# mLSTM phase of a hybrid decoder step: gated output made in four column pieces between units, six dense chunks of the last head pair held back, another matmul order in a unit

## The reference, cut to what matters

```python
def mlstm_mixer(xn, w_in, b_i, b_f, head_gain, w_out, C0, n0, m0, chunk):
    proj = (xn @ w_in).astype(F32)
    q, k, v, o, ig, fg = jnp.split(proj, cuts, axis=-1)
    ...
    h, C, n, m = mlstm_chunkwise(q, k, v, log_i, log_f, C0, n0, m0, chunk)
    h = h * lax.rsqrt(jnp.mean(h * h, axis=-1, keepdims=True) + EPS) * head_gain
    out = (jax.nn.sigmoid(o) * h.reshape(B, S, H * DV)).astype(xn.dtype) @ w_out
```

## Time and profile before

| | |
|---|---|
| median of three runs | 2530.48 us |
| profiled execution, its own time | 2529.18 us |
| its span | 2527.4 us |
| PE busy | 2442.5 us (97%), 15530 matmul instructions |
| DVE busy | 1164.1 us (46%) |
| ACT busy | 651.7 us (26%) |
| POOL busy | 160.1 us (6%) |
| chain that ended last | PE 90%, DVE 5% |

### The profile page before, as it was taken

How to read it: one execution, slowest core, us unless ns; L and a number is a source line. 1 busy time by engine, 2 the same in 40 slices (tenths; PEclk the granted TensorE clock), 3 DMA queues, 4 the chain that set the end, 5 groups by cost and what they waited for, 6 DMA issues and landing times.

```text
span 2527.4 us, 36895 instructions
## 1 busy us (share of the span) xinstructions
PE 2442.5 (97%) x15530; PEld 2330.6 (92%) x15530; DVE 1164.1 (46%) x2023; ACT 651.7 (26%) x1080; POOL 160.1 (6%) x208
## 2 busy tenths in 40 slices
PE   6999999997999999999999999999999999999998
PEld 6889898887999999999999977869999999999997
DVE  5545545566434334333336665466433333333333
ACT  3232222233212112112113354253212112112113
POOL 3000000002000000000002011012000000000002
PEclk8999999998999999999999999999999999999999
DMA  3212121101111111111111311101111111111111
GB/s 104 50 36 64 47 65 37 43 22 39 42 51 42 43 51 45 41 50 51 42 49 55 96 30 49 34 18 34 43 50 51 43 43 50 43 50 43 42 51 69
DMA packets 177416, 120.55 MB, mean 48 GB/s; under 512 B 23623, under 2 KB 173044, under 8 KB 177220
## 3 DMA queue, kind: packets, MB, share of 16 engines
q1 hardware_dynamic: 177108, 118.10, 16.0%
q10 hardware_dynamic: 144, 0.02, 0.0%
HBM read 110.94 MB, written 12.33 MB: 49 GB/s over the span
## 4 chain that ended last, share of the span: by engine, by line
PE 90%; DVE 5%; ACT 1%; issue 1%; DMA 1%; POOL 1%; SPq 0%; DVEq 0%; ACTq 0%
PE acc L1592 59%; PE acc L1672 5%; PE acc L1674 4%; PE acc L1673 4%; PE acc L1869 3%; PE acc L1871 3%; PE acc L1870 3%; PE acc L1888 1%; PE acc L1911 1%; PE acc L1899 1%; PE acc L1728 1%; DVE w_lo L1032 1%; PE acc L1695 1%; DVE rstd L1050 1%; PE acc L1713 1%
## 5 line engine op out<-in xcount | busy, mean ns | idle before, releaser
L1592 PE MATMUL acc<-x_hi,w_hi 128*128 128x352 f32 x1560 | 341.0, 327 | 15.4 <-DVE x_lo L1038 6.6
L1063 DVE TENSOR_TENSOR x_res<-x_res,acc 128x1056 f32<-128x1056 f32 x128 | 160.4, 1253 | 413.6 <-PE acc L1592 413.6
L683 ACT ACTIVATE w_hi<-w_raw 128x1024 fp32r<-128x1024 f32 x180 | 189.2, 1051 | 609.4 <-PE acc L1592 527.6
L1592 PE MATMUL acc<-x_lo,w_hi 128*128 128x352 f32 x1560 | 338.0, 325 | 0.0
L1592 PE MATMUL acc<-x_hi,w_lo 128*128 128x352 f32 x1560 | 337.8, 324 | 0.0
L1592 PE MATMUL acc<-h_hi,w_hi 128*128 128x352 f32 x1536 | 332.1, 324 | 0.0
L1592 PE MATMUL acc<-h_hi,w_lo 128*128 128x352 f32 x1536 | 331.1, 323 | 0.0
L1592 PE MATMUL acc<-h_lo,w_hi 128*128 128x352 f32 x1536 | 330.6, 323 | 0.0
L1592 PEld LDWEIGHTS acc<-x_hi,w_hi 128*128 128x128 f32 x1560 | 266.9, 190 | 18.7 <-issue 13.6
L1592 PEld LDWEIGHTS acc<-x_hi,w_lo 128*128 128x128 f32 x1560 | 269.6, 189 | 0.0
L1592 PEld LDWEIGHTS acc<-x_lo,w_hi 128*128 128x128 f32 x1560 | 266.7, 189 | 0.0
(11 more groups left out here) (265 smaller groups left out, 3103.5 us busy)
## 6 DMA issues: line engine op xcount, KB each, us to landing
w_raw<-in_w_up SPq DMA_DIRECT2D x64, 512.0 KB
w_raw<-in_w_down SPq DMA_DIRECT2D x64, 512.0 KB
w_raw<-in_w_mlstm_in SPq DMA_DIRECT2D x24, 512.0 KB
x_in<-in_x_prompt SPq DMA_DIRECT2D x8, 512.0 KB, 3.9
w_raw<-in_w_mlstm_out SPq DMA_DIRECT2D x8, 512.0 KB
w_raw<-in_w_q SPq DMA_DIRECT2D x16, 256.0 KB
w_raw<-in_w_attn_out SPq DMA_DIRECT2D x16, 256.0 KB
out_y_prompt<-y_out SPq DMA_DIRECT2D x8, 512.0 KB, 2.6
```

The lines of the kernel that those rows point to most:

```text
L683: nc.scalar.activation(w_hi[:, s.parity], w_raw[:, s.parity], ACT.Copy).then_inc(hi_split, 1)
L1063: V.tensor_tensor(blocks(x_res[:, k]), blocks(x_res[:, k]), group(o), ALU.add).then_inc(out_taken, 1)
L1592: last = T.matmul(out[:, b], w[:, k, m], x[:, TN * b:TN * b + TN], start=(k == 0 and i == 0), stop=(k == k_chunks - 1 and i == 2))
```

## The change

The six last chunks of the last pair (`HELD`) leave its windows and run after its units, before its own `out` slabs. The gated output is made in four pieces of columns (0:384, 384:768, 768:1024, samples), each by `gate`, `y_high`, `y_low`; `y_hi` gets two buffers. In the last `out` slabs DVE prepares row r-1 behind the sum of row r. On PE `part1`, `part2` and the sample unit's `part3` issue the same matmuls in another order.

```diff
+HELD = 6
+PIECES = [slice(0, 3 * LC), slice(3 * LC, 6 * LC), slice(6 * LC, SEQ), slice(SEQ, TOK)]
 def window(pr, step):
-    lo, n = PERIOD[pr], PERIOD[pr + 1] - PERIOD[pr]
+    lo, n = PERIOD[pr], PERIOD[pr + 1] - PERIOD[pr] - (HELD if pr == NPAIR - 1 else 0)
...
# ACT
-                def y_high(v):
+                def y_high(i):
+                    act.wait_ge(y_done, 4 * pr + i + 1)
                     for e in range(2):
...
                     if c == NCH:
-                        if pr > 0:
-                            act.wait_ge(blk_ready, evacuated(("out", pr - 1, 1)))
-                        act.wait_ge(y_done, 2 * pr + 1)
-                        y_high(slice(0, SEQ))
+                        y_high(2)
                     dense(window(pr, 3 * c + 5))
-                act.wait_ge(y_done, 2 * pr + 2)
-                y_high(slice(SEQ, TOK))
+                    if c in (6, 7):
+                        y_high(0 if c == 6 else 1)
+                y_high(3)
...
-            dense(range(PERIOD[NPAIR], PERIOD[NPAIR] + 8))
+            dense(range(PERIOD[NPAIR] - HELD, PERIOD[NPAIR] + 8))
# DVE, in dense
                             mark(x_final)
-                            prepare(1, FFN0, row)
+                            if row > 0:
+                                prepare(1, FFN0, row - 1)
+                            if row == KD - 1:
+                                prepare(1, FFN0, row)
# DVE, in units
                         heads_out(c - 1)
-                    update(c)
                     if c == NCH:
                         dve.wait_ge(ht_taken, t0 + NCH)
-                        dve.wait_ge(sig_done, 2 * pr + 2)
-                        gate(slice(0, SEQ))
+                        gate(2)
+                    update(c)
                     dense(window(pr, 3 * c + 4))
                     normalise(c)
+                    if c in (6, 7):
+                        dve.wait_ge(ht_taken, t0 + c)
+                        dve.wait_ge(sig_done, 2 * pr + 2)
+                        gate(0 if c == 6 else 1)
+                    if c in (7, 8):
+                        y_low(0 if c == 7 else 1)
                     if c + 2 < NT:
                         exponents(c + 2)
...
                 heads_out(NCH)
                 dve.wait_ge(ht_taken, t0 + NT)
-                gate(slice(SEQ, TOK))
-                y_low(slice(0, SEQ), 2 * pr + 1)
-                y_low(slice(SEQ, TOK), 2 * pr + 2)
+                gate(3)
+                y_low(2)
+                y_low(3)
...
+            dense(range(PERIOD[NPAIR] - HELD, PERIOD[NPAIR]))
             dve.wait_ge(n_ready, 1)
# PE, in dense
-                            pe.wait_ge(yl_ready, 2 * pr + 2)
+                            pe.wait_ge(yl_ready, 4 * pr + 3)
...
+                        if kind == "out" and k == 0 and b == 2:
+                            pe.wait_ge(yl_ready, 4 * pr + 4)
# PE, part1
                     T.transpose(acc[0:n, 0, 0:P], own[:, 1, cc], ident[:])
                     for e in range(2):
-                        T.matmul(acc[0:n, 0, P + P * e:P + P * e + n], head_sel[:, e, 0:n], mx_all[:, cc], start=True, stop=True)
+                        T.transpose(acc[0:n, 2, P * e:P * e + P], own[:, 2 + e, cc], ident[:])
                     for e in range(2):
-                        x = T.transpose(acc[0:n, 2, P * e:P * e + P], own[:, 2 + e, cc], ident[:])
+                        x = T.matmul(acc[0:n, 0, P + P * e:P + P * e + n], head_sel[:, e, 0:n], mx_all[:, cc], start=True, stop=True)
# PE, part2
-                    pe.wait_ge(a_ready, t + 1)
                     pe.wait_ge(v_ready, t + (2 if c + 1 < NT else 1))
                     if c > 0:
                         pe.wait_ge(c_ready, t)
                     if t > 0:
+                        pe.wait_ge(i_ready, t)
+                    if c < NCH:
+                        for e in range(2):
+                            h = slice(DK * e, DK * e + DK)
+                            T.matmul(acc[0:n, 2 + e, 0:DV + 1], own[h, 0, cc], c_aug[pr % 2][h], start=True, stop=True)
+                    pe.wait_ge(a_ready, t + 1)
+                    if t > 0:
                         pe.wait_ge(nd_ready, t)
-                        pe.wait_ge(i_ready, t)
                     for e in range(2):
                         x = T.matmul(acc[0:P, 0, P + (DV + 1) * e:P + (DV + 1) * (e + 1)], amat[0:n, e], v_aug[0:n, c % 2, e],
                                      start=True, stop=True)
-                    if c < NCH:
...
# PE, part3 of the sample unit: (e outer, b inner) becomes (b outer, e inner)
-                        for b in range(DEC_B):
-                            T.matmul(acc[h, 2 + b // 4, DV * (b % 4):DV * (b % 4) + DV], kw_b[:, b, h], v_aug[0:n, c % 2, e, 0:DV],
-                                     start=True, stop=True)
-                        x = T.matmul(acc[h, 1, 0:DEC_B], k_w[0:n, c % 2, h], s_rows[:], start=True, stop=True)
+                    else:
+                        for b in range(DEC_B):
+                            for e, h in enumerate(halves):
+                                T.matmul(acc[h, 2 + b // 4, DV * (b % 4):DV * (b % 4) + DV], kw_b[:, b, h],
+                                         v_aug[0:n, c % 2, e, 0:DV], start=True, stop=True)
+                        for h in halves:
+                            x = T.matmul(acc[h, 1, 0:DEC_B], k_w[0:n, c % 2, h], s_rows[:], start=True, stop=True)
# PE, after the pairs
-            dense(range(PERIOD[NPAIR], PERIOD[NPAIR] + 16))
+            dense(range(PERIOD[NPAIR] - HELD, PERIOD[NPAIR] + 16))
```

More of the change, by code:

```diff
@@ L243, in build @@
         pair = [sb(f"pair{i}", [P, 6, TOK], where=phase) for i in range(2)]
-        y_hi = sb("y_hi", [P, 2, TOK], F32R, where=phase)
+        sb("above_pairs", [P, 2, TOK], where=phase)
         c_old = sb("c_old", [P, DEC_B, DV + 1], where=phase)
@@ L272, in build @@
         phase = ExitStack()
-        y_lo = []
+        y_hi, y_lo = [], []
         for i in range(2):
-            sb(f"below_y{i}", [P, 4, TOK], where=phase)
+            y_hi.append(sb(f"y_hi{i}", [P, 2, TOK], F32R, where=phase))
+            sb(f"below_y{i}", [P, 2, TOK], where=phase)
             y_lo.append(sb(f"y_lo{i}", [P, 2, TOK], F32R, where=phase))
@@ L780, in values_and_exps @@
                     nc.scalar.activation(expd[0:n, :, 0:n], dmat[0:n, :, 0:n], ACT.Exp).then_inc(e_ready, 1)
-                def y_high(v):
+                def y_high(i):
+                    act.wait_ge(y_done, 4 * pr + i + 1)
                     for e in range(2):
-                        g = HEAD * KD + 2 * pr + e
-                        x = nc.scalar.activation(y_hi[:, e, v], pair[pr % 2][:, 4 + e, v], ACT.Copy, scale=gains[:, g:g + 1])
+                        g, v = HEAD * KD + 2 * pr + e, PIECES[i]
+                        x = nc.scalar.activation(y_hi[pr % 2][:, e, v], pair[pr % 2][:, 4 + e, v], ACT.Copy, scale=gains[:, g:g + 1])
                     x.then_inc(yh_ready, 1)
@@ L1307, in heads_out, with gate, y_low @@
                                   ).then_inc(ht_taken, 1)
-                def gate(v):
+                def gate(i):
                     for e in range(2):
+                        v = PIECES[i]
                         x = V.scalar_tensor_tensor(own[:, 4 + e, v], own[:, 4 + e, v], 1.0, own[:, 2 + e, v], ALU.add, ALU.mult)
                     x.then_inc(y_done, 1)
-                def y_low(v, n):
-                    dve.wait_ge(yh_ready, n)
+                def y_low(i):
+                    dve.wait_ge(yh_ready, 4 * pr + i + 1)
                     for e in range(2):
-                        g = HEAD * KD + 2 * pr + e
+                        g, v = HEAD * KD + 2 * pr + e, PIECES[i]
                         x = V.scalar_tensor_tensor(y_lo[pr % 2][:, e, v], own[:, 4 + e, v], gains[:, g:g + 1],
-                                                   y_hi[:, e, v].bitcast(F32), ALU.mult, ALU.subtract)
+                                                   y_hi[pr % 2][:, e, v].bitcast(F32), ALU.mult, ALU.subtract)
                     x.then_inc(yl_ready, 1)
@@ L1662, in dense @@
                         if kind == "out":
-                            pe.wait_ge(yl_ready, 2 * pr + 2)
+                            pe.wait_ge(yl_ready, 4 * pr + 3)
                     hi, lo = (w[:, s % 2].rearrange("p (k m) -> p k m", k=n_k)[:, kk, P * n:P * n + P] for w in (w_hi, w_lo))
-                    mh, ml = (x_hi[:, kk], x_lo[:, kk]) if kind == "in" else (y_hi[:, kk], y_lo[pr % 2][:, kk])
+                    mh, ml = (x_hi[:, kk], x_lo[:, kk]) if kind == "in" else (y_hi[pr % 2][:, kk], y_lo[pr % 2][:, kk])
                     for b in range(TB):
@@ L1729, in part2 @@
                                      start=True, stop=True)
-                    if c < NCH:
-                        for e in range(2):
-                            h = slice(DK * e, DK * e + DK)
```

(17 more changed lines are left out.)

## The result

The changed kernel takes 2499.94 us in the median of four runs (2495.87 to 2501.94), the kernel before 2531.79 us (also four); the ratio is 0.9882, 95% interval 0.9867 to 0.9896. The execution on the page has a span of 2496.7 us, 30.7 less than before.

What follows compares the result with a forecast made beforehand. PE was taken to bound the kernel (busy 97% of the span), except in a tail where DVE and ACT decide. Terms -6.4 - 4.8 - 1.1 + 1.9 - 2.5 = -12.9 us gave 2517.5 us for the median, range 2506 to 2526.

Steps and rivals of the forecast that it cites:

- The sample unit's part3: PE's 32 small matmuls per pair, alternating column halves: 1.6 us a pair less, -6.4 us for four.
- part2: PE's small products after `scores`: one change of shape goes, 0.15 us in each of 32 units, -4.8 us.
- y_low no longer last: DVE at the end of a pair: less y_lo before the next pair's `exponents(0)`, so shorter PE waits, -1.1 us.
- The last pair: Last pair with six held chunks: -10.0 us from hole and half clock, +11.9 from new waits and clock drops, net +1.9.
- the held rows: Held chunks after the last unit: DVE comes to their rows late, PE waits for banks, 1.9 us.
- prepare a row later: Last `out` slabs: x_lo made later but held by POOL's sum, so only first rows and one split gain, -2.5 us.
- tail works as drawn: Rival: no new waits of weight in units 6 to 8, no blocking at x_lo; sum -25, 2505 us; chance 0.2.
- the waits in units 6 to 8: Last pair: PE waits 2.9 us at `scores(8)`, 2.3 at `sample_states`, and 1.9 for banks after unit 8.
- the blocking of x_lo: Last `out` slabs: x_lo on DVE held by POOL's sum, so a row takes at least 3.84 us.
- The order does nothing: Rival: `part3` and `part2` on PE keep their pace; 2528.8 us, within 0.2%; chance 0.13.
- the alternation costs: Rival: each change of column half in `part3` costs 0.15 us, +9 in all; 2533 to 2537 us; chance 0.06.

Runs made afterwards that it cites:

- a_old_orders: The changed kernel with `part1`, `part2` and `part3` in the order of the kernel before; ratio 0.9966 (0.9953 to 0.9979).
- a_short_sums: The changed kernel with POOL's seven sums of squares before the first MLP over 2 of the 1056 columns; 2495.69 us, ratio 0.9882.

## Why the prediction was wrong

The way was right and nearly each mechanism is in the trace; the sizes were not. By the steps of the prediction:

- *The sample unit's part3*, -6.4 us: right. 1.96 us per part3, 4 x 1.6 = 6.3 us, and -6.8 us when done alone.
- *part2*, -4.8 us: **this term was mis-sized most, with the clock below**. I took 0.15 us for the one change of shape that I counted as gone. Two go, since the amat product now has a matmul of its own 128-row shape behind it, and each is worth 0.19: 28 x 0.38 + 4 x 0.18 = 11.3 us, and 0.8 more in the dense matmul behind it. The earlier trace rows had it: amat took 0.64 us in front of a state product, where scores and state took 0.42. The fixed 0.15 us that I drew from two groups of another width was no price of a change. The upper bound given, 0.3 us a unit, was also too low. `part1`, put at 0, costs 1.1 us.
- *y_low no longer last*, -1.1 us: the wait at the last pair's first `scores` is 1.77 us in after, as before, with a chunk less in front of it; the other two (0.7 us in sum) are gone. But the term came out with the wrong sign. I had the moved pieces hidden in pairs 0 to 2, and in pairs 1 and 2 they cost two new waits of 0.72 us for an `in` block (1.4 us, a_old_orders has them too): +0.7 us and not -1.1.
- *The last pair*, net +1.9 us: the waits were right (2.8 and 2.2 us for 2.9 and 2.3), the held rows cost 0.46 + 0.87 us for 1.9. **The clock was wrong.** I charged 3.6 us for two drops behind the new waits and kept the old stretches at 472 and 485 us. In both traces of after only three dense matmuls at half clock are left, at 526 us, behind the 2.8 us wait, and its 2.2 us wait slows only `sample_states` (3.6 us for 1.9). Half clock costs before some 6 us more than after (7.3 on dense matmuls, 1.3 back on small ones), where my sum had it 0.4 dearer in after. This is the second part of the missing 17 us. Which half of the change brings it is open: with the orders alone 47 dense matmuls at half clock stay, with the tail alone 53, in one trace each, but by the clock of all runs the orders alone leave it where it was (0.984 to 0.987) and the tail alone reaches after's in four runs of twelve.
- *prepare a row later*, -2.5 us: the mechanism was right (x_lo held by POOL's sum, 2.1 to 3.1 us). The walk had the second w_lo wait for a sum; it ran clear (1.21 us at 576.34), and the early rows ran at PE's pace of 2.87 us. From the first row's sum to the last it took 26.1 us, against 33.1 before. Of these 7.0 us 4.9 are PE's waiting (8.2 to 3.3 us), where I had 2.5 for the whole term; the other 2.2 are 17 dense matmuls at half clock behind the 4.15 us wait of the earlier trace rows, counted with the clock. Alone the edit gives -4.3 us (interval -6.8 to -1.5).
- *Sum*: between -12.9 and the -27.3 us of the stretch lie 14.4. By the rows they are -7.3 and +1.1 (`part2` and `part1`), -6.4 (clock: 6 gained, and not 0.4 lost), -1.5 (waits of the last pair: even, where I had +1.5), -2.4 (rows) and +1.8 (y_low): -14.7. The experiments cut it in two: I had -11.2 for the orders and -1.7 for the rest, and alone they give -18.4 (interval -21.5 to -15.2) and -8.6 (-11.9 to -5.3). Each half was too small by some 7 us. A further 2.9 us between the two profiled executions lie ahead of the first unit and are scatter of the runs.

Of the rivals, *tail works as drawn* (2505) came nearest in number, for another reason: the waits in units 6 to 8 and the blocking of x_lo were all there. *The order does nothing* and *the alternation costs* are out.

## What to carry to other kernels

Where small matmuls of different row counts stand between large ones, count in a timeline how often the shape changes and lay like beside like: 0.19 us a change, 11 us over 32 units here for nothing but order. Small products on different halves of the array should alternate (6 us here). Work that an engine does early to shorten a tail belongs behind what the bounding engine waits for at that moment, not in front of it: the same pieces two statements later gave another 3 us.

## What the runs showed of the hardware that I had not expected

- The same twelve small matmul instructions take 1.11, 1.49 or 2.09 us by their order alone; a product's own time depends on what stands behind it (amat: 0.46 us before a dense matmul, 0.64 before a 64-row one).
- Eight 32x128 products on each column half take 3.54 us as two runs of eight, 2.56 in runs of four, 1.96 alternating.
- DVE and POOL hold each other up when both read SBUF with two inputs: x_lo 1.32 us alone and up to 3.12 beside a sum (a_short_sums shows the cause), the sum 2.47 us alone and 3.25 behind an x_lo or a w_lo (read from the times alone).
- The clock is worth as much as an edit: 59 dense matmuls at half clock against 3 are 7.3 us, and the one place that after has comes back in its second trace. Which wait leads to a drop could not be told: the last pair's first `scores` waits 1.8 us in both kernels, and is followed by half clock in one only, and a drop of 17 dense matmuls at 208 us in a_old_orders follows no wait at all.
